# Delta rule's inverse: the transposed factor of each level made by a transpose and a copy

## The reference

```
L = jnp.where(strict, jnp.einsum('nbhcd,nbhsd->nbhcs', k_beta, k) * decay, 0.0)
A = L + jnp.eye(CHUNK, dtype=f32)
sol = lax.linalg.triangular_solve(A, rhs, left_side=True, lower=True, unit_diagonal=True)
```

## Time and profile before

| | |
|---|---|
| median of three runs | 773.28 us |
| the profiled execution | 773.29 us |
| its span | 771.5 us |
| TensorE, matmuls | 748.5 us busy, 97% of the span |
| TensorE, weight loads | 688.8 us, 89% |
| VectorE | 574.5 us, 74% |
| ScalarE | 393.8 us, 51% |
| GpSimd | 26.2 us, 3% |
| DMA | 148.94 MB, mean 193 GB/s |
| granted clock of TensorE | 0.998 of full speed |

### The profile page before, as it was taken

One profiled execution on the slowest core, in us unless ns is written; L12 is line 12 of the kernel. 1 busy time (PEld: TensorE's weight loads), 2 busy tenths in 40 slices (PEclk: granted clock), 3 DMA queues, 4 the chain that ended last, 5 costly groups with the idle time before them and its releaser, 6 DMA issues.

```text
span 771.5 us, 13336 instructions
## 1 busy us (share of the span) xinstructions
PE 748.5 (97%) x5280; PEld 688.8 (89%) x5280; DVE 574.5 (74%) x964; ACT 393.8 (51%) x665; POOL 26.2 (3%) x31
## 2 busy tenths in 40 slices
PE   7999999889999999999999999999999999999996
PEld 7988999877999999999979887799889999999995
DVE  5758889776776766778677998767857767766776
ACT  5472233665544444434474444557547556555655
POOL 0030000100000000000013000000010000000000
PEclk9999999999999999999999999999999999999999
DMA  7744345354489988789615523365335655555441
GB/s 298 260 146 168 110 151 179 129 172 138 146 326 354 331 289 282 269 282 366 232 49 199 187 87 109 110 219 183 128 128 181 219 198 169 182 205 186 165 137 55
DMA packets 40526, 148.94 MB, mean 193 GB/s; under 512 B 4496, under 2 KB 4624, under 8 KB 40080
## 3 DMA queue, kind: packets, MB, share of 16 engines
q1 hardware_dynamic: 39600, 142.91, 53.7%
q10 hardware_dynamic: 864, 5.18, 1.7%
HBM read 147.02 MB, written 1.05 MB: 192 GB/s over the span
## 4 chain that ended last, share of the span: by engine, by line
PE 75%; DVE 15%; ACT 6%; issue 3%; POOL 1%; DMA 1%; DVEq 0%; SPq 0%; ACTq 0%
PE bank L1034 13%; PE bank L1037 13%; PE bank L1035 13%; PE bank L1092 6%; PE bank L1093 6%; PE bank L1090 6%; PE bank L1068 5%; PE bank L1217 4%; DVE wlo L1447 4%; DVE arena L1453 3%; PE bank L1081 3%; DVE XN L1453 2%; DVE arena L1447 2%; ACT arena L1995 2%; ACT whi L1995 2%
## 5 line engine op out<-in xcount | busy, mean ns | idle before, releaser
L1034 PE MATMUL bank<-hh,whi 128*128 128x256 f32 x1000 | 286.3, 286 | 0.2
L1035 PE MATMUL bank<-hl,whi 128*128 128x256 f32 x1000 | 282.8, 283 | 0.0
L1037 PE MATMUL bank<-hh,wlo 128*128 128x256 f32 x1000 | 282.8, 283 | 0.0
L1447 DVE TENSOR_TENSOR wlo<-raw,whi 128x1024 fp32r<-128x1024 f32 x202 | 242.3, 1231 | 27.9 <-ACT whi L1995 27.5
L1995 ACT ACTIVATE whi<-raw 128x1024 fp32r<-128x1024 f32 x202 | 202.3, 1047 | 27.7 <-DMA raw<-w_dram 21.8
L1034 PEld LDWEIGHTS bank<-hh,whi 128*128 128x128 f32 x1000 | 191.5, 192 | 4.3 <-issue 2.0
L1035 PEld LDWEIGHTS bank<-hl,whi 128*128 128x128 f32 x1000 | 191.6, 192 | 1.5
L1037 PEld LDWEIGHTS bank<-hh,wlo 128*128 128x128 f32 x1000 | 191.5, 192 | 0.0
L1453 DVE SCALAR_TENSOR_TENSOR arena<-bank,cols,arena 128x255 f32<-128x255 f32 (+3 forms) x138 | 58.9, 480 | 28.9 <-ACT arena L1995 27.1
L1995 ACT ACTIVATE arena<-bank 128x256 f32<-128x256 f32 (+2 forms) x65 | 26.8, 421 | 89.9 <-PE bank L1037 71.0
L1092 PE MATMUL bank<-wlo,fh 128*128 128x512 f32 x176 | 69.2, 393 | 1.1 <-DVE wlo L1447 1.1
(11 more groups left out here) (176 smaller groups left out, 893.9 us busy)
## 6 DMA issues: line engine op xcount, KB each, us to landing
raw<-w_dram SPq DMA_DIRECT2D x268, 512.0 KB, 4.8
arena<-rows_dram ACTq DMA_DIRECT2D x1, 1792.0 KB, 9.5
X<-x_dram SPq DMA_DIRECT2D x2, 512.0 KB, 4.5
arena<-rows_dram ACTq DMA_DIRECT2D x1, 1024.0 KB, 12.9
arena<-bias_dram ACTq DMA_DIRECT2D x1, 1024.0 KB, 16.1
out_dram<-X SPq DMA_DIRECT2D x4, 256.0 KB, 2.1
const<-const_dram ACTq DMA_DIRECT2D x1, 640.0 KB, 3.9
arena<-bias_dram ACTq DMA_DIRECT2D x1, 512.0 KB, 4.8
```

Source lines behind the costliest of these rows:

```text
L1034: e.matmul(o, a, hh[:, k, :], start=(k == 0), stop=False)
L1035: e.matmul(o, a, hl[:, k, :], start=False, stop=False)
L1037: ins = e.matmul(o, wlo[:, s, k * 128:k * 128 + 128], hh[:, k, :], start=False, stop=(k == 7))
L1447: return e.tensor_tensor(out, a, b, op)
```

## The change

U of a level is no longer a product. A new step lev_u stands behind lev_y of the next level: TensorE transposes the new Tm, four heads to a bank and two blocks, and ScalarE copies the bank to Um. lev_tu becomes lev_t, which has the products for T alone in levels 1 to 5, and for U alone in level 6. VectorE's subtraction for U stays in level 6 only. The number of fills is the same and their order another.

```diff
             P.step("lev_y", lev)
+            if lev > 1:
+                for b in range(2):
+                    P.fill(f"U{lev - 1}{b}")
+                P.step("lev_u", lev - 1)
             yield
             for b in range(2):
-                if lev < LEVELS - 1:
-                    P.fill(f"T{lev}{b}")
-                P.fill(f"U{lev}{b}")
-            P.step("lev_tu", lev)
+                P.fill(f"U{lev}{b}" if lev == LEVELS - 1 else f"T{lev}{b}")
+            P.step("lev_t", lev)
             yield
...
+            def lev_u(lev):
+
+                for b in range(2):
+                    p = open_bank(f"U{lev}{b}")
+                    wait_after(f"T{lev}{b}")
+                    for h in range(4):
+                        ins = e.transpose(p[:, h * 128:h * 128 + 128], Tm[:, b, h, :], K("ident"))
+                    filled(ins, f"U{lev}{b}")
+
+            def lev_t(lev):
                 last = lev == LEVELS - 1
                 for b in range(2):
                     open_bank(f"U{lev}{b}" if last else f"T{lev}{b}")
...
                         wait_after(f"U{lev - 1}{b}")
-                    if not last:
+                    if last:
+                        heads(f"U{lev}{b}", lambda h: Ym[:, b, h, :], lambda h: Um[:, b, h, :])
+                    else:
                         heads(f"T{lev}{b}", lambda h: Um[:, b, h, :], lambda h: Ym[:, b, h, :])
-                        open_bank(f"U{lev}{b}")
-                    heads(f"U{lev}{b}", lambda h: Ym[:, b, h, :], lambda h: Um[:, b, h, :])
...
-            def lev_tu(lev):
+            def lev_t(lev):
                 for b in range(2):
                     if lev < LEVELS - 1:
...
                         freed(tt(Tm[:, b, :, :], Tm[:, b, :, :], v3(F[f"T{lev}{b}"].bank), ALU.subtract), f"T{lev}{b}")
+                        continue
                     wait_full(f"U{lev}{b}")
-                    if lev == 1:
-                        w.wait_ge("um0", b + 1)
-                    else:
-                        wait_after(f"U{lev - 1}{b}")
+                    wait_after(f"U{lev - 1}{b}")
                     freed(tt(Um[:, b, :, :], Um[:, b, :, :], v3(F[f"U{lev}{b}"].bank), ALU.subtract), f"U{lev}{b}")
...
+            def lev_u(lev):
+                for b in range(2):
+                    name = f"U{lev}{b}"
+                    p = wait_full(name)
+                    freed(af(Um[:, b, :, :], v3(F[name].bank), ACT.Copy), name)
```

More of the change, by code:

```diff
@@ L1421, in _ @@
                 "turn_ba": turn_ba, "lam": lam_, "norms": norms, "decay": decay, "kk": kk, "kq": kq, "lev_first": lev_first,
-                "lev_y": lev_y, "lev_tu": lev_tu, "vturn": vturn, "solve": solve, "cross": cross,
+                "lev_y": lev_y, "lev_t": lev_t, "lev_u": lev_u, "vturn": vturn, "solve": solve, "cross": cross,
                 "values_la": values_la, "turn_la": turn_la,
@@ L1964, in _ @@
                 "split_ba": split_ba, "conv": conv, "ba": ba, "lam": lam_, "gates": gates, "norms": norms,
-                "factors": factors, "em": em, "kk": kk, "kq": kq, "lev_mask": lev_mask, "lev_first": lev_first, "lev_y": lev_y, "lev_tu": lev_tu,
+                "factors": factors, "em": em, "kk": kk, "kq": kq, "lev_mask": lev_mask, "lev_first": lev_first, "lev_y": lev_y, "lev_t": lev_t,
                 "vturn": vturn, "cross": cross, "la_sums": la_sums, "la_rows": la_rows, "head_la": head_la, "squares_od": squares_od, "stats": stats, "head": head, "scores1": scores1, "soft1": soft1, "mix1": mix1,
@@ L2321, in _ @@
                 "start": start, "hi": hi, "square": sumsq, "squares": sumsq, "sumsq": sumsq, "root": root, "rows": rows, "tv": tv, "th": th, "split_ba": split_ba,
-                "conv": conv, "silu": silu, "lam": lam_, "vd": vd_, "qk": qk, "z": z, "gates": gates, "dsq": dsq, "decay": decay,
+                "conv": conv, "silu": silu, "lev_u": lev_u, "lam": lam_, "vd": vd_, "qk": qk, "z": z, "gates": gates, "dsq": dsq, "decay": decay,
                 "solve": solve, "values_la": values_la, "head_la": head_la, "stats": stats, "table": table, "spread_od": spread_od, "head": head, "scores1": scores1, "soft1": soft1, "turn1": turn1,
```

## The result

The changed kernel takes 768.61 us (median of four, 768.19 to 769.02) against 773.39 for the kernel before: ratio 0.9935, 95% interval 0.9924 to 0.9947. That is 4.8 us less, and 0.2 us from the 768.8 that was forecast. The profiled execution took 768.96 us, its span 766.9 (4.6 us less than before).

The account below looks back on a forecast made before the run. The prediction took the stretch around the inverse as bound by TensorE, with VectorE close behind. Its terms, -8.93 + 4.50 - 0.90 + 0.80 = -4.53 us, gave 768.8 us from 773.28, range 767.2 to 771.7.

Parts of the forecast that it names:

- TensorE's term: Levels 1 to 5: 80 product records dropped, 8.93 us less; 5 x 8 transposes added, 4.50 us more; net 4.4 less.
- The bank at level 5: TensorE's wait at level 5 for the bank of attention step 4's scores goes: 0.9 us less (0 to 0.9).
- the shorter queue: At level 5, VectorE's queue is shorter by two subtractions of level 4, named beside the bank order; no separate size.
- The bank at level 3: T of level 3, block 0, waits for ScalarE's copy of the attention product: 0.8 us more (0 to 1.8).
- "Does it last": After the levels, TensorE's 2.4 us wait for ScalarE moves with TensorE's progress; the gain is kept whole to the end.
- The copies cost nothing: ScalarE's ten copies of U, 5.9 us more work, cost nothing by themselves, as ScalarE has room.
- the half units as cover: One or two half units, about 1.4 us each, between a level's transposes and its T hide ScalarE's copies.
- VectorE was costed at nothing: Ten subtractions taken from VectorE, 6 to 6.8 us less work there, count for nothing by themselves.
- Rival 1: Three more levels pay 0.8 us each for a bank or copy as level 3 does: 771.2 us; chance 0.08.
- Rival 2: VectorE is a second bound of 85 to 130 us; its relief gives more, at best 767.3 us; chance 0.10.
- Rival 3: Attention's own chain sets the first part's end; the wait at 142 grows by the saving: 773.2 us; chance 0.08.
- Rival 5: The clock falls to 1.2 GHz for a level, through the transposes: 780 us or more; chance 0.02.

Follow-up runs that it names:

- Experiment 1: Changed kernel with each of its 40 transposes done as a full float32 product of Tm with the identity; 773.39 us, 0.9998 of the kernel before.
- experiment 2: Kernel before, without VectorE's ten subtractions for U of levels 1 to 5, ScalarE copying these products to Um instead; 773.44 us, 0.9999 of the kernel before.
- experiment 4: Changed kernel with each level's transposes and copies put directly ahead of the next T, behind the half unit; 778.23 us, 1.0071 of the kernel before.
- experiment 3: Changed kernel with the ten copies to Um on VectorE in place of ScalarE; 771.84 us, 0.9982 of the kernel before.
- experiment 5: Changed kernel run again as it is, as the measure of later runs; 768.75 us median, 0.9951 of the kernel before.
- Experiment 6: Changed kernel with the two T fills of level 3 in the other order; 767.37 us, 0.9927 of the kernel before.
- experiment 11: Changed kernel with level 3's T fills exchanged, level 6's second fill passing over a bank, and ten unused products in TensorE's 2.65 us wait; 768.68 us.
- experiment 7: Changed kernel with level 3's T fills exchanged and level 6's second fill passing over the attention product's bank; 770.15 us, 0.9953 of the kernel before.

## Why the prediction was right

**TensorE's term** was right in both parts: five halves of 16 records less at 1.79 us, five times eight transposes more at 0.87 to 0.88 in place of the 0.90 taken (4.4 in place of 4.50). Together -4.5 us. Experiment 1 gives back 4.17 of the 4.40 us over the levels with nothing but this term changed; the bank terms nearly cancel each other.

**The bank at level 5** was forecast at 0.90 and was right at 0.92, and it is the order that does it, as said, and not the shorter queue, which I had named beside it (experiment 2: 0.1). **The bank at level 3** was forecast at 0.8 and took 0.66, by the chain that was named: copy, whi, copy (ScalarE, changed kernel, in order of time; the first row is both copies of U and that of turn1):

```profile
92.96 1.36 ACT L2004 ACTIVATE arena<-bank 128x512 f32<-128x512 f32 x3 [3.57 <-PE bank L1260]
94.19 0.41 ACT L2004 ACTIVATE arena<-arena,small 128x128 f32<-128x128 f32 x1
94.49 1.07 ACT L2004 ACTIVATE whi<-raw 128x1024 fp32r<-128x1024 f32 x1
95.49 0.38 ACT L2004 ACTIVATE arena<-bank 128x256 f32<-128x256 f32 x1
```

**What was left out:** 0.33 us at level 6. U's second fill has the same bank behind the same attention product in both orders. Before, TensorE waited for nothing there; in the changed kernel it arrives earlier against ScalarE, and the wait shows. With it the terms give -8.93 + 4.4 - 0.92 + 0.66 + 0.33 = -4.46, against 4.40 measured over the levels. The forecast of -4.53 is as near as it is because the 0.33 left out was nearly made up by three terms that came out 0.26 better than forecast together. That is luck, and so are the 0.3 us of the total that lie ahead of the levels.

**"Does it last"** was right: the wait of 2.65 us moved with TensorE's progress and did not grow, and 200 to 400 us is as it was.

**The copies cost nothing** was right as a result. Its reason, the half units as cover, was at most part of it: experiment 4 lost that and the place ahead of the exponentials, and paid 9 us over the levels. The prediction did not name that place as what protects the copies. VectorE was costed at nothing as well; in experiment 3, whose copies load VectorE about as the subtractions had, the levels take 2 us more, so its relief is a condition of the gain.

**The other rivals.** Rival 1: two waits came, at levels 3 and 6, and no more. Rival 2: VectorE's relief by itself gives 0.1 us (experiment 2). Rival 3: the wait did not grow. Rival 5, the clock: the granted clock is 1.00 between 70 and 130 us, where the transposes are, in the ten profiles that have them in the changed kernel's place. By the statement in the Trainium skill ("TensorE: Matmul & The Clock Gate", "Part 4: PE-mode transpose") that the full clock does not engage for transposes it might have fallen; groups of eight transposes among products did not show that (1.00). What the clock did fall behind were TensorE's waits of 2.15 us and more, and the two behind the levels stood in the kernel before too.

## What to carry to other kernels

Where TensorE is the bound and both a matrix and its transpose are kept up, make one by products and the other by a transpose: in float32 it took half of the product's time here (0.109 us against 0.223). Put the copy of it into the in-order queue ahead of anything that waits for a third engine: in experiment 4 the copies were ready and ScalarE idle for some 3 us behind such a wait. When fills take banks in turn, walk the new order by hand: each wait of TensorE that went or came between the two kernels was one of these banks. And where launches scatter by more than the change is worth, compare a fixed stretch of the trace, here the levels, beside the medians.

## What the runs showed of the hardware

I had not expected single launches of one kernel on one core to differ by 2 us and more (experiment 5: 768.29 to 772.95 us, at a mean granted clock of 0.998 to 0.992). Two sources show in the profiles.

One is TensorE's waits. It ran at 2.4 GHz almost throughout, but behind a wait of 2.15 to 2.65 us it came back at 1.2 GHz in some executions, seen as eight records in 1.78 us in place of 0.97, and in others not. A fall cost 0.9 to 1.2 us. Ten and eight small products with no use, put into these two waits, removed it (0.999 in five of five).

The other is the start. The first products of L1019 are the same in every kernel. Experiment 6 and experiment 11, weight loads in order of time:

```profile
7.23 2.08 PEld L1019 LDWEIGHTS bank<-const,XN 128*128 128x128 f32 x16 [0.35 <-DVE XN L1461]
...
7.60 3.27 PEld L1023 LDWEIGHTS bank<-const,XN 128*128 128x128 f32 x16 [0.37 <-DVE XN L1465]
```

Eight loads of this line take 0.86 us at 185.47 us in the changed kernel, so 16 in 3.27 us are nearly half as fast, as at the lower level of the clock. These two executions have the earliest and the latest start of the levels, 68.12 and 69.89 us, and 1.2 of the 1.8 us between them are in these 16 records. That the clock does it is inferred from the records' pace: the granted clock of the view is 1.00 there.

A saving of 1 us elsewhere can so be hidden by which launches are slow: experiment 7 was 1.1 us better over the levels and 1.4 us worse by its median than experiment 5.
